# A two-layer block kernel: per-layer gates computed with tokens on the partitions in two token blocks, their normed rows turned back, and the first shared values moved ahead of the keys

## The chip, the core and the metric

The kernel runs on one NeuronCore of a Trainium2 chip. The metric is device time in microseconds from one launch to its end, so lower is better. Five instruction streams run beside each other and meet only at semaphores: TensorE (matmul), VectorE, ScalarE, GpSimd, and SyncE, which here only issues DMAs. Each stream is strictly in order: an instruction that waits holds everything behind it.

## What is computed

The kernel runs two blocks of a small language model over 256 tokens (272 with 16 meta tokens in the first block) of width 1024, batch 1, all in float32. The change touches the second block only. Per layer i that block does:

```python
for i in range(2):
    h = rms_norm(x, g_pre_mix[i])
    if i == 0:
        mix = short_conv_mixer(h, ...)
    else:
        k, v = shared_kv(x, g_kv, w_kv)     # rms_norm(x, g_kv) @ w_kv, split in keys and values
        mix = diff_attention(h, k, v, ...)  # 8 heads, two softmaxes a head, subtracted
    x = x + rms_norm(mix, g_post_mix[i])
    ffn = conv_ffn(rms_norm(x, g_pre_ffn[i]), ...)   # up to 2 * 2816, causal conv of width 3, silu gate, down
    x = x + rms_norm(ffn, g_post_ffn[i])
    gate = sigmoid(rms_norm(x, g_pre_ple[i]) @ w_gate[i])          # 1024 x 1024
    x = x + rms_norm(gate * (p[i] @ w_proj[i]), g_post_ple[i])     # p[i]: 256 tokens x 256
```

Weights come in float32 and are used as a rounded high part plus a remainder, and so are the activations: each product is three matmuls (high weight with high activation, high with low, low with high).

## The kernel before

**Layout.** The residual `X` and the normed inputs `UH` (high) and `UL` (low) have features on the partitions and tokens along the free axis. A root mean square is taken outside the products: the gain is applied in `split_hi`/`split_lo` (line 540), the products run on the unnormed rows, and the token's reciprocal root is multiplied in when a product is evicted. `root_begin`, `root_sum` and `root_end` sum squares over the partitions with one-column matmuls (line 462), `root_sqrt` (line 506, ScalarE) and `root_recip` (line 513, VectorE) make the reciprocal, `root_spread` (line 520) spreads it over all partitions, `root_keep` (line 528) copies it. `preload` (line 532) evaluates a function on one column so that its table is loaded early. `keep_going` (line 402) runs products of ones on TensorE that nobody reads.

**Weights.** All weights are one stream of units of up to 128 x 1024, in the order of `weight_units`. SyncE loads unit n into one of four `RAW` buffers as soon as unit n-4 has been split. ScalarE (`act_split`, line 346) rounds it into one of seven `WH` buffers, once the unit seven before has been marked `used` by TensorE; VectorE (`dve_split`, line 353) makes the remainder `WL`. TensorE waits for `wl`. The places of all splits in the two streams are written out by hand. `products` (line 368) makes one 128-row output tile of 24 matmuls, 256 tokens wide; `first_products` (line 413) makes four such tiles side by side, k by k, so that it can follow the arrival of `UL` k by k.

**PSUM banks.** The eight PSUM banks are handed out by the class `Banks`, in the order in which TensorE's stream is written. `take` gives the next bank round the ring, skipping one that is held, and makes TensorE wait for the event that frees the bank's last contents; `put` names the bank itself and waits in the same way. `root_banks` takes two neighbours and marks the second as free after `root_sqrt` (`rs`). `hold` keeps the first of the pair out of the ring until the next `root_sum`; `go_on` moves the ring's place. In `tensor_ffn` this place matters:

```python
elif u == 2:
    # m == 0: b = banks.take(...)            then root_sum takes two banks
    # m == 1: b = banks.put(t, banks.at["root", prev], ...)
...
if (u, m) == (3, 0):
    banks.go_on((banks.at["root", prev] + 1) % 8)
```

Tile (u, m) of the up projection is evicted by VectorE into `FZ` (line 2322, event `fz`), in order (0,0), (0,1), (1,0) and so on, between weight splits and the convolution's taps. Before, in layer 0, the pair of the root of `sco` is in banks 6 and 7, the five embedding tiles of `embed(0, 5)` in 0 to 4, the first four up tiles in 5, 7, 0 and 1, tile (2,0) in 2, the root of `ffn0` in 3 and 4, tile (2,1) in 6 and tile (3,0) in 5.

**The per-layer embedding.** `embed(j0, j1)` in `tensor_ffn` makes the tiles of p @ w_proj: tiles 0 to 4 at the entrance of the feed-forward, 5 to 7 before the gate. ScalarE copies them to `MM2` (line 2176). Then the gate runs as four pairs of feature tiles: VectorE multiplies by the reciprocal root (line 2349), ScalarE takes the sigmoid (line 2247), VectorE multiplies by `MM2` (line 2355), ScalarE squares. The norm of the result is the start of the next stage: `tensor_diff` (layer 0) or `tensor_end` (layer 1) fills with `keep_going`, sums, spreads, and `add_normed` (lines 1902 and 1905) or `vector_end` (lines 2817 and 2819) adds to `X`.

**Keys, values and attention.** `tensor_diff` makes the eight key tiles first, four of them by `first_products`, with the root of `kv`; then a loop over eight steps s does query s, the scores of head s-1, `value(s)` (line 2450, half of a 256-column value block), and attention of head s-2. VectorE multiplies keys and queries by the root on eviction (lines 2676 and 2694). After the loop the output projection makes its first four tiles in banks 0 to 3 and takes the next banks round the ring for the other four; ScalarE squares (line 1858) and copies (line 1860) each output tile.

## Time and profile before

| what | us |
|---|---|
| three timed executions | 1263.52, 1260.85, 1262.09 |
| their median | 1262.09 |
| span of the profiled execution | 1261.9 |
| TensorE busy in it | 1231.6 (98%) |
| VectorE busy | 908.1 (72%) |
| ScalarE busy | 737.1 (58%) |
| mean granted TensorE clock | 0.994 of full speed |

The span runs from the first to the last instruction of the profiled execution; it is 0.2 us from the median of the timed ones. A timeline row reads: start, duration, engine, line, operation, output and inputs, shapes, count, and in brackets the idle time ahead of it with the engine that ended it. Matmuls are pipelined, so the duration of one is longer than its distance to the next; the distance is what it costs. On the page, the line of a group gives its busy time and the mean duration of one instruction in ns.

### The profile page before, as it was taken

How to read it: one execution, taken by the hardware profiler on the slowest of the kernel's cores; microseconds unless marked ns; L12 is line 12 of the kernel's file. 1: busy time of each engine (PE TensorE's matmuls, PEld its weight loads, DVE VectorE, ACT ScalarE, POOL GpSimd, SP SyncE). 2: the span in 40 equal slices, each digit the busy share in tenths (PEclk: the TensorE clock that was granted, in tenths of full speed). 3: DMA queues.
4: the chain of work that ended last, by engine and by line, in shares of the span. 5: the costliest groups of instructions: out<-in, count | busy, mean ns of one | idle time of the engine just before them, and what ended most of it. 6: DMA issues, size and time to landing. Idle time of an engine off the chain costs nothing.

```text
span 1261.9 us, 24318 instructions
## 1 busy us (share of the span) xinstructions
PE 1231.6 (98%) x10110; PEld 1206.4 (96%) x10110; DVE 908.1 (72%) x1571; ACT 737.1 (58%) x1257; POOL 6.4 (1%) x16
## 2 busy tenths in 40 slices
PE   8999999999999999999999999999999999999997
PEld 8889799999999999999999999999888899999997
DVE  6896566665446776444876899966788768999656
ACT  6753456664445765334555666655766866665655
POOL 1000000000000000000000000000000000000000
PEclk9999999999999999999999999999899999999999
DMA  7223244555552655553663666574364236665640
GB/s 275 72 101 105 64 164 148 192 181 180 174 168 98 216 186 185 184 184 126 218 195 119 193 194 199 159 238 134 120 225 159 89 117 192 193 189 188 215 141 34
DMA packets 59753, 205.51 MB, mean 163 GB/s; under 512 B 6739, under 2 KB 9340, under 8 KB 59516
## 3 DMA queue, kind: packets, MB, share of 16 engines
q1 hardware_dynamic: 57536, 201.21, 49.0%
q10 hardware_dynamic: 2108, 2.75, 0.7%
q8 instruction: 80, 1.31, 0.4%
q14 instruction: 29, 0.24, 0.1%
HBM read 202.87 MB, written 1.06 MB: 162 GB/s over the span
## 4 chain that ended last, share of the span: by engine, by line
PE 85%; DVE 8%; ACT 4%; issue 1%; DMA 1%; DVEq 0%; ACTq 0%
PE PS L368 69%; PE PS L413 6%; DVE WL L353 2%; PE PS L380 2%; DMA RAW<-wpack 1%; ACT WH L346 1%; PE PS L462 1%; PE PS L2450 1%; ACT EE L2608 1%; PE PS L520 1%; PE PS L2517 0%; PE PS L688 0%; DVE X L1905 0%; ACT L532 0%; PE PS L402 0%
## 5 line engine op out<-in xcount | busy, mean ns | idle before, releaser
L353 DVE TENSOR_TENSOR WL<-RAW,WH 128x1024 fp32r<-128x1024 f32 (+2 forms) x387 | 460.6, 1195 | 211.3 <-ACT WH L346 210.8
L346 ACT ACTIVATE WH<-RAW 128x1024 fp32r<-128x1024 f32 (+2 forms) x387 | 392.3, 1033 | 218.6 <-PE PS L368 184.8
L368 PE MATMUL PS<-UH,WH 128*128 128x256 f32 (+1 forms) x1464 | 415.7, 284 | 7.6 <-DVE WL L353 3.8
L368 PE MATMUL PS<-UL,WH 128*128 128x256 f32 (+1 forms) x1464 | 414.9, 283 | 0.0
L368 PE MATMUL PS<-UH,WL 128*128 128x256 f32 (+1 forms) x1464 | 414.7, 283 | 0.0
L368 PEld LDWEIGHTS PS<-UH,WH 128*128 128x128 f32 x1464 | 276.6, 189 | 8.6 <-issue 3.4
L368 PEld LDWEIGHTS PS<-UH,WL 128*128 128x128 f32 x1464 | 276.9, 189 | 0.0
L368 PEld LDWEIGHTS PS<-UL,WH 128*128 128x128 f32 x1464 | 275.2, 188 | 0.0
L368 PE MATMUL PS<-HL,WH 128*128 128x272 f32 (+1 forms) x512 | 145.8, 285 | 0.0
L368 PE MATMUL PS<-HH,WH 128*128 128x272 f32 (+1 forms) x512 | 145.6, 284 | 0.0
L368 PE MATMUL PS<-HH,WL 128*128 128x272 f32 (+1 forms) x512 | 145.4, 284 | 0.0
L368 PE MATMUL PS<-FH,WH 128*128 128x256 f32 x352 | 98.5, 280 | 0.0
L368 PE MATMUL PS<-FL,WH 128*128 128x256 f32 x352 | 98.5, 280 | 0.0
L368 PE MATMUL PS<-FH,WL 128*128 128x256 f32 x352 | 98.5, 280 | 0.0
L368 PEld LDWEIGHTS PS<-HH,WL 128*128 128x128 f32 x512 | 96.6, 189 | 0.0
L368 PEld LDWEIGHTS PS<-HL,WH 128*128 128x128 f32 x512 | 96.3, 188 | 0.0
L368 PEld LDWEIGHTS PS<-HH,WH 128*128 128x128 f32 x512 | 96.1, 188 | 0.0
L413 PE MATMUL PS<-UH,WH 128*128 128x256 f32 (+1 forms) x240 | 68.7, 286 | 1.5 <-DVE UL L540 1.2
L413 PE MATMUL PS<-UL,WH 128*128 128x256 f32 (+1 forms) x240 | 67.6, 282 | 0.0
L413 PE MATMUL PS<-UH,WL 128*128 128x256 f32 (+1 forms) x240 | 67.6, 282 | 0.0
L368 PEld LDWEIGHTS PS<-FH,WH 128*128 128x128 f32 x352 | 66.2, 188 | 0.0
L368 PEld LDWEIGHTS PS<-FL,WH 128*128 128x128 f32 x352 | 66.2, 188 | 0.0
(409 smaller groups left out, 2066.1 us busy)
## 6 DMA issues: line engine op xcount, KB each, us to landing
RAW<-wpack SPq DMA_DIRECT2D x361, 512.0 KB, 4.2
RAW<-wpack SPq DMA_DIRECT2D x18, 384.0 KB, 3.5
RAW<-wpack SPq DMA_DIRECT2D x6, 256.0 KB, 2.7
C<-cst SPq DMA_DIRECT2D x1, 1072.0 KB, 5.9
HB<-bias_rows ACTq DMA_DIRECT2D x1, 1024.0 KB, 5.3
out<-X SPq DMA_DIRECT2D x4, 256.0 KB, 2.3
X<-xin ACTq DMA_DIRECT2D x2, 272.0 KB, 6.0
X<-xin SPq DMA_DIRECT2D x2, 272.0 KB, 5.9
```

The source lines that it names most:

```text
L346: a.e.activation(WH[n % NH][:, 0:w], RAW[n % NR][:, 0:w], ACT.Copy).then_inc(*a.mark("wh", n))
L353: v.e.tensor_tensor(WL[n % NH][:, 0:w], RAW[n % NR][:, 0:w], WH[n % NH][:, 0:w].bitcast(f32), ALU.subtract).then_inc(*v.mark("wl", n))
L368: ins = t.e.matmul(o, part(n, hw, kw, a, b), x(kx), start=first and not i and not p, stop=last and i == len(kcs) - 1 and p == 2)
L380: ins = t.e.matmul(o, x(kx), part(n, hw, kw, 0, w), start=not i and not p, stop=i == len(kcs) - 1 and p == 2)
L413: ins = t.e.matmul(PS[:, b, 0:w], part(n, hw, k, 0, 128), x_(k), start=k == 0 and p == 0, stop=k == 7 and p == 2)
L462: return t.e.matmul(o, src[:, m, a:z], ONE[:, 0:1], start=start, stop=stop)
L520: ins = t.e.matmul(PS[:, b, a:z], rooted(st, x).to_broadcast([128, 128]), ID[:, 0:z - a], start=True, stop=True)
L2450: ins = t.e.matmul(PS[:, b, 0:256], x[:, k, 128 * i:128 * i + 128], part(n, hw, kw, 0, 256), start=k == 0 and p == 0, stop=k == 7 and p == 2)
L2608: ins = a.e.activation(e, e, ACT.Exp, bias=s[:, 2 * i + m:2 * i + m + 1], scale=-1.0, accum_out=s[:, 4 + 2 * i + m:5 + 2 * i + m])
```

## The change

- **Units.** The gate's weights come as eight units of two k-slices x 512 columns instead of eight of eight k-slices x 128 columns. The first 512 value columns come as four such units ahead of the keys; keys 4 to 7 take the places of value halves 0 to 3 in the loop. The embedding's weights are cut at columns 512 and 768.
- **Embedding.** `embed` uses 128 tokens as the stationary operand and 256 features as the moving one; six tiles instead of five are made at the entrance of the feed-forward, two instead of three before the gate. `MR` is the token-major view of `MM2`.
- **Gate.** Tokens on the partitions: the reciprocal root becomes the per-partition scale of the sigmoid, which reads PSUM directly. Columns 0 to 511 of both token blocks are made side by side, with `root_sum` after k = 5 of 8; then columns 512 to 1023 of block 0, then of block 1. The sum of squares comes from accumulators on ScalarE and VectorE. Root, reciprocal and scaling of block 0 follow while TensorE makes block 1, and `gate_turned` turns the normed rows of block 0 back with eight transposes, placed inside the products of block 1. `gate_added` multiplies by the gain and adds to `X`.
- **Layer 0's follow-up.** `tensor_diff` begins with the value products of block 0, in which the transposes of block 1 stand ahead of k = 6; then the value products of block 1, the bias product, and keys 0 to 3. Fillers, sum and spread of the root of `ple0` are gone.
- **Layer 1's end.** Block 1's second half is made in two column halves; its reciprocal root goes into a diagonal matrix with which eight matmuls turn and scale at once. The output leaves in eight DMAs of 128 KB instead of four of 256 KB.

The core of the diff:

```diff
         else:
-            proj("k", "w_kv_2", None, 0, 1024)
-            for g in range(4):
-                for m in range(2):
-                    proj("q", "w_q_2", 0, 256 * g + 128 * m, 256 * g + 128 * m + 128)
-                    u.append(("v", "w_kv_2", None, list(range(4 * m, 4 * m + 4)), cols(1024 + 256 * g, 1280 + 256 * g)))
+            pairs_of_rows("v", "w_kv_2", None, 1024, 1536)
+            proj("k", "w_kv_2", None, 0, 512)
+            for h in range(8):
+                proj("q", "w_q_2", 0, 128 * h, 128 * h + 128)
+                if h < 4:
+                    proj("k", "w_kv_2", None, 512 + 128 * h, 640 + 128 * h)
+                else:
+                    m, c = h % 2, 1024 + 256 * (h // 2)
+                    u.append(("v", "w_kv_2", None, list(range(4 * m, 4 * m + 4)), cols(c, c + 256)))
...
             root_spread(t, prev, S)
-            embed(2, 5)
+            embed(2, 6)
...
             root_end(t, f"f{layer}", 1, S)
-            embed(5, 6)
+            embed(6, 7)
             root_spread(t, f"f{layer}", S)
-            embed(6, 8)
-            keep_going(t, 2, f"f{layer}")
+            embed(7, 8)
+            keep_going(t, 8, f"f{layer}")
...
+            def gate_rows(h, k, blocks_, c0=0, c1=512):
+                n, kw = n0 + 4 * h + k // 2, k % 2
+                t.wait_ge("wl", n)
+                t.wait_ge("ul", st, k)
+                for i in blocks_:
+                    if k == 0:
+                        banks.take(t, ("gate", layer, i, h, c0), ("sig", layer, i, h, int(c1 == 512)))
...
+            for k in range(8):
+                n = gate_rows(0, k, (0, 1))
+                if k == 5:
+                    root_sum(t, st, 0, S, ("rs", st))
             for u in range(4):
+                sig.also(("used", n0 + u), ("gate", layer, 1, 0, 0))
+            for k in range(8):
+                gate_rows(1, k, (0,))
+            if layer == 0:
+                for k in range(8):
+                    if k == 6:
+                        gate_turned(t, layer, 0)
+                    gate_rows(1, k, (1,))
...
+            gate_sigmoid(a, layer, 0, 0, 0, 512)
+            gate_sigmoid(a, layer, 1, 0, 0, 512)
+            act_split(a, n0 + NH + 2)
             gate_square(0)
+            act_split(a, n0 + NH + 3)
             gate_square(1)
+            act_split(a, n0 + NH + 4)
+            gate_sigmoid(a, layer, 0, 1, 0, 512)
+            preload(a, ACT.Sqrt, 61)
+            gate_root(a, layer, 0)
+            preload(a, ACT.Sigmoid, 62)
+            gate_scale_first(a, layer, 0)
...
         def tensor_diff(t):
-            keep_going(t, 10)
-            root_begin(t, "ple0", 1, S, ("mr", "kv", 6))
-            banks.hold(("root", "ple0"))
-            keep_going(t, 8)
-            root_end(t, "ple0", 1, S)
-            root_spread(t, "ple0", S)
+            for i in range(2):
+                b = banks.take(t, ("v", 0, i), ("v", 0, i))
+                for k in range(8):
+                    if (i, k) == (0, 6):
+                        gate_turned(t, 0, 1)
...
+            spare = banks.at["nt", 0, 0]
+            b = banks.put(t, spare, ("gr",), ("gr0",))
...
+            for j in range(4):
+                key(j, banks.take(t, ("k", j), ("kh", j)) if j != 2 else banks.put(t, spare + 1, ("k", j), ("kh", j)))
+                if j == 1:
+                    root_sum(t, "kv", 0, S, ("rk", "kv"))
+                if j == 2:
                     root_spread(t, "kv", S)
...
+                if s < 4:
+                    key(4 + s, banks.put(t, BV + s % 2, ("k", 4 + s), ("kh", 4 + s)))
+                    return
...
+            parts(0, 0, 4)
+            gate_product(v, 0, 1, 1, 0, 512)
+            gate_squares(v, 0, 1)
+            dve_split(v, n0)
+            parts(0, 4, 6)
+            gate_recip(v, 0, 1)
+            gate_scale_second(v, 0, 1)
+            parts(0, 6, 8)
+            dve_split(v, n0 + 1)
+            parts(1, 0, 8)
...
-            key(0)
-            key(1)
-            dve_split(v, n0 + NH + 2)
-            key(2)
-            key(3)
-            dve_split(v, n0 + NH + 4)
-            for j in range(4, 8):
+            for j in range(4):
                 key(j)
+                dve_split(v, n0 + NH + 1 + j)
```

On ScalarE the squares of `kv`, the copy of the bias row, the eight query inputs (`XH`) with four weight splits among them, `root_sqrt` of `kv`, `root_keep` and then the two copies of the first values follow in this order. `parts(i, a, b)` is, per feature tile, `gate_added` and then the low part of the key and value input; its high part is on ScalarE.

## Rows read from the trace of the kernel before

**Rows 1.** The page: busy time of the engines, the two costliest groups

```profile
PE 1231.6 (98%) x10110; PEld 1206.4 (96%) x10110; DVE 908.1 (72%) x1571; ACT 737.1 (58%) x1257; POOL 6.4 (1%) x16
...
L353 DVE TENSOR_TENSOR WL<-RAW,WH 128x1024 fp32r<-128x1024 f32 (+2 forms) x387 | 460.6, 1195 | 211.3 <-ACT WH L346 210.8
...
L346 ACT ACTIVATE WH<-RAW 128x1024 fp32r<-128x1024 f32 (+2 forms) x387 | 392.3, 1033 | 218.6 <-PE PS L368 184.8
```

**Rows 2.** TensorE's timeline at the first convolved feed-forward: start us, us, engine, line, operation

```profile
679.93 0.36 PE L413 MATMUL PS<-UH,WH 128*128 128x256 f32 x1
...
697.99 0.28 PE L368 MATMUL PS<-UH,WH 128*128 128x256 f32 x1
...
701.81 0.36 PE L368 MATMUL PS<-UH,WH 128*128 128x256 f32 x1 [0.82 <-DVE WL L353]
```

**Rows 3.** Timelines there, then of the second layer: VectorE's evictions into FZ, TensorE

```profile
697.18 0.76 DVE L2322 TENSOR_TENSOR FZ<-PS,RR 128x256 f32<-128x256 f32 x2 [1.31 <-ACT RR L528]
...
708.95 0.41 DVE L2322 TENSOR_TENSOR FZ<-PS,RR 128x256 f32<-128x256 f32 x1
...
1059.70 0.41 DVE L2322 TENSOR_TENSOR FZ<-PS,RR 128x256 f32<-128x256 f32 x1
...
1052.57 0.36 PE L368 MATMUL PS<-UH,WH 128*128 128x256 f32 x1 [0.82 <-DVE WL L353]
```

**Rows 4.** ScalarE's timeline there: two copies of embedding tiles

```profile
680.36 0.64 ACT L2176 ACTIVATE MM<-PS 128x256 f32<-128x256 f32 x2
```

**Rows 5.** The gate stage of layer 0, timelines of TensorE and VectorE

```profile
873.69 0.36 PE L413 MATMUL PS<-UH,WH 128*128 128x256 f32 x1 [0.59 <-DVE UL L540]
...
885.37 0.58 PE L462 MATMUL PS<-ONE,ACC 128*128 128x1 f32 x4
...
884.79 0.43 DVE L449 TENSOR_TENSOR ACC<-ACC 128x256 f32<-128x256 f32 x1
...
890.06 0.69 DVE L2355 TENSOR_TENSOR MM<-MM,TMA 128x512 f32<-128x512 f32 x1
```

**Rows 6.** The same stage on ScalarE, timeline

```profile
886.26 1.28 ACT L532 ACT_TABLE_LOAD   x1
...
887.56 0.20 ACT L532 ACTIVATE SMALL<-EPS 128x1 f32<-128x1 f32 x1
...
889.40 1.29 ACT L2247 ACTIVATE TMA<-TMA 128x512 f32<-128x512 f32 x2
```

**Rows 7.** TensorE's timeline elsewhere: 512-column products, four transposes and the product after

```profile
148.73 0.39 PE L380 MATMUL PS<-WH,CL 128*128 128x512 f32 x1
...
148.95 0.39 PE L380 MATMUL PS<-WL,CH 128*128 128x512 f32 x1
...
987.61 0.60 PE L2490 MATMUL PS<-ID,MM 128*128 128x128 f32 x4
...
987.97 0.37 PE L368 MATMUL PS<-XH,WH 128*128 128x256 f32 x1
```

**Rows 8.** TensorE's timeline after the gate of layer 0

```profile
925.44 0.71 PE L520 MATMUL PS<-ID,RS 128*128 128x128 f32 x4 [1.61 <-DVE RS L513]
...
934.92 0.39 PE L368 MATMUL PS<-XH,WH 128*128 128x256 f32 x1
...
941.20 0.39 PE L368 MATMUL PS<-XH,WH 128*128 128x256 f32 x1 [0.47 <-DVE QH L2694]
```

**Rows 9.** Table by stretch: busy per engine, then granted clock, DMA share, GB/s

```profile
898.70:902.10 3.40, 2.62 (x24) 2.45 (x22) 2.87 (x10) 2.50 (x6) 0.00 (x0) 1.00 0.05 12
...
905.50:908.90 3.40, 3.40 (x14) 2.63 (x13) 3.15 (x7) 2.28 (x5) 0.00 (x0) 0.50 0.49 162
```

**Rows 10.** Attention's output tiles, timelines of TensorE and ScalarE

```profile
1013.77 0.28 PE L368 MATMUL PS<-UH,WH 128*128 128x256 f32 x1
...
1017.39 0.50 ACT L1860 ACTIVATE M<-PS,G 128x256 f32<-128x256 f32 x1
```

**Rows 11.** VectorE's timeline: the kernel's last addition

```profile
1258.41 0.69 DVE L2819 TENSOR_TENSOR X<-X,MM 128x512 f32<-128x512 f32 x1
```

More of the change, by code:

```diff
@@ L36, in rows, with pairs_of_rows @@
                 u.append((key, name, idx, list(range(k, k + 4)), cols(c, c + 256)))
+    def pairs_of_rows(key, name, idx, a, b):
+        for c in range(a, b, 512):
+            for k in (0, 2, 4, 6):
+                u.append((key, name, idx, [k, k + 1], cols(c, c + 512)))
     def blocks(n):
@@ L2089, in embed @@
                 for j in range(j0, j1):
-                    x, j_, last = (0, 0, 3) if j < 4 else (1, 4, 4) if j < 5 else (2, 5, 7)
-                    n, at = unit_at["ple", 3 * layer + x], 128 * (j - j_)
+                    i, x, at = j % 2, (0, 0, 1, 2)[j // 2], (0, 256, 0, 0)[j // 2]
+                    n = unit_at["ple", 3 * layer + x]
                     b = banks.take(t, ("ple", layer, j), ("pe", layer, j))
-                    products(t, PS[:, b, 0:S], n, [(0, 0), (1, 1)], at, at + 128,
-                             lambda k: PH[:, k, :], lambda k: PL[:, k, :], lambda k: ("ul", "p", layer)).then_inc(
-                                 *t.mark("ple", layer, j))
-                    if j == last:
+                    t.wait_ge("wl", n)
+                    t.wait_ge("ul", "p", layer)
+                    for k in range(2):
+                        for p, (y, hw) in enumerate(((PH, 1), (PL, 1), (PH, 0))):
+                            ins = t.e.matmul(PS[:, b, 0:256], y[:, k, 128 * i:128 * i + 128], part(n, hw, k, at, at + 256),
+                                             start=k == 0 and p == 0, stop=k == 1 and p == 2)
+                    ins.then_inc(*t.mark("ple", layer, j))
+                    if j in (3, 5, 7):
                         sig.also(("used", n), ("ple", layer, j))
@@ new lines, in gate_rows @@
+            def gate_rows(h, k, blocks_, c0=0, c1=512):
+                n, kw = n0 + 4 * h + k // 2, k % 2
+                t.wait_ge("wl", n)
+                t.wait_ge("ul", st, k)
+                for i in blocks_:
+                    if k == 0:
+                        banks.take(t, ("gate", layer, i, h, c0), ("sig", layer, i, h, int(c1 == 512)))
+                    b = banks.at["gate", layer, i, h, c0]
+                    for p, (x, hw) in enumerate(((UH, 1), (UL, 1), (UH, 0))):
+                        ins = t.e.matmul(PS[:, b, c0:c1], x[:, k, 128 * i:128 * i + 128], part(n, hw, kw, c0, c1),
+                                         start=k == 0 and p == 0, stop=k == 7 and p == 2)
+                    if k == 7:
+                        ins.then_inc(*t.mark("gate", layer, i, h, c0))
+                return n
@@ new lines, in tensor_ffn, with gate_turned @@
+            for u in range(4, 8):
+                sig.also(("used", n0 + u), ("gate", layer, 1, 1, 256 * layer))
+        def gate_turned(t, layer, i):
+            b = banks.take(t, ("nt", layer, i), ("x2", AFTER[layer], i, 7), 2)
+            t.wait_ge("m", f"ple{layer}", i)
+            t.wait_ge("mr", f"ple{layer}", i)
+            for j in range(8):
+                ins = t.e.transpose(PS[:, b + j // 4, 128 * (j % 4):128 * (j % 4) + 128], MR[:, i, 128 * j:128 * j + 128], ID[:, :])
+                if j % 4 == 3:
+                    ins.then_inc(*t.mark("nt", layer, i, j // 4))
@@ L2254, in last_step @@
-            def last_step():
-                ple = f"ple{layer}"
-                for m in range(2):
-                    a.wait_ge("gz", layer, 3, m)
-                    a.e.activation(TMA[:, 2 + m, 0:S], TMA[:, 2 + m, 0:S], ACT.Sigmoid).then_inc(*a.mark("sig", layer, 3, m))
-                a.wait_ge("acc", ple, 1)
-                a.free["sq", 1] = ("sum", ple)
-                for m in range(2):
-                    a.wait_ge("pg", layer, 3, m)
-                    a.e.activation(SQ[1][:, m, 0:S], MM2[:, 6 + m, :], ACT.Square).then_inc(*a.mark("sq", ple, 3, m))
-                sig.also(("sq", ple, 3), ("sq", ple, 3, 1))
@@ L2567, in scalar_diff @@
             root_sqrt(a, "kv", S)
-            act_split(a, n0 + NH + 1)
             root_keep(a, "kv", 0, S)
-            act_split(a, n0 + NH + 4)
+            a.wait_ge("rr", "kv")
+            for i in range(2):
+                a.wait_ge("dif", "v", 0, i)
+                a.e.activation(V[:, i, 0:512], PS[:, banks.at["v", 0, i], :], ACT.Copy, scale=rooted("kv", 1 + i)).then_inc(
+                    *a.mark("v", 0, i))
+            act_split(a, n0 + 4 + NH)
             scalar_embed(a, 1)
```

313 lines of the change are left out of this document (175 added, 138 removed).

## The prediction

> **What bounds the kernel now.** I read the page first: TensorE is busy 98% of the span, VectorE 72%, ScalarE 58% [rows 1]. So TensorE's own work sets the time, and a change pays only if it takes work or idle time from TensorE. Next I read TensorE's waits and its timeline. They show few gaps: 0.82 us at each feed-forward entrance [rows 2, 3], 0.59 us ahead of the gate [rows 5], 1.61 and 0.47 us around keys and queries [rows 8]. The larger loss is hidden in the busy time: after each gate the stream holds fillers, one-column sums and a spread instead of products. In layer 0 this fills the ten microseconds of [rows 9], and there the granted clock falls to 0.50, from 2.4 to 1.2 GHz, after a stretch in which TensorE was busy 2.62 of 3.40 us, partly with one-column sums. The change aims at this, and at the tail, where VectorE ends at 1259.10 [rows 11]. Last I went through the diff for every wait that TensorE gets, which includes the hand-out of PSUM banks: a stream with 98% busy loses what it waits.
>
> **Part 1, the sixth embedding tile at the entrance of the feed-forward.** It looks free: one tile of six matmuls changes places. But it takes a bank. Counting on from front: the root of `sco` stays in 6 and 7 (6 held), the embedding now takes 0 to 5, the first four up tiles 7, 0, 1, 2, tile (2,0) bank 3, the root of `ffn0` 4 and 5, and `put` places tile (2,1) in 6. The hold has just ended, so the ring gives tile (3,0) the next bank: 6 again. Before it was 5, whose contents had left at 697.5. Now (3,0) waits for the eviction of (2,1). The sixth FZ eviction in VectorE's order is that one, at 708.95, ended 709.36 [rows 3], while TensorE is ready for (3,0) at 697.99 [rows 2]. Two smaller shifts come on top: tile (1,1) now lies in bank 2 and waits for the copy of embedding tile 2, the first of the pair at 680.36, so the products begin at 680.8 and not at 679.93 [rows 2, 4]; of these 0.9 us, 0.7 stay, and the spread, root copy and evictions follow TensorE, so they shift too. Then (3,0) starts at 710.2 and (3,1) one tile later. A tile is 24 matmuls at 0.12 us (96 of them fill 873.69 to 885.37 [rows 5]), 2.85 us: 713.05, against 701.81 [rows 2], which already holds the old 0.82 us wait. **Cost 11.2 us.** Nothing gives it back: behind this point TensorE runs without a gap and the splits it needs are even further ahead. The second layer repeats it if the root of `do` and the embedding lie the same way. By my count `lam` ends in bank 1, so attention's last output tiles take 2 to 5, that root 6 and 7, the embedding again 0 to 5. With 1059.70 and 1052.57 [rows 3] the sum is 1059.70 + 0.41 + 0.7 + 0.1 + 2.85 - 1052.57 = **11.2 us.**
>
> **Part 2, gate of layer 0 to the first query.** I laid the new order out by hand on the three engines from 873.69 on. A 512-column matmul costs 0.23 us [rows 7] against two of 0.12, so 96 in the gate and 48 for the values save about 1 us in all. Eight transposes cost 0.8 us (0.36 for four [rows 7]); sigmoid, copies and squares of 512 columns 0.65, a table load with its dummy 1.46 [rows 6], a product of 512 columns 0.69 [rows 5], a weight split 1.03 on ScalarE and 1.2 on VectorE [rows 1]. The 128-token additions and remainders are not in the trace; 0.3 us each is my estimate, between half of and the whole 0.41 of 256 columns [rows 3]. The waits that result on TensorE:
> - `root_sum` after k = 5 is reached at 882.2, but needs the sum of squares, which ends at 885.22 [rows 5]. Before, it stood behind k = 7 and waited for next to nothing. **3.1 us.** The first half ends at 888.6.
> - The transposes of block 0 need its scaling. On ScalarE, behind the end of the first half, stand a split, two sigmoids, two squares, three more splits, the third sigmoid and two table loads around the root: ready at 900.2. **1.9 us.** The gate ends at 902.5.
> - Value product k = 4 of block 0 needs a remainder on VectorE that stands behind block 1's product, its squares and a split, and an input on ScalarE behind split, sigmoid and table load: 908.4. **3.2 us.**
> - Block 1 of the values starts behind one more split on both: 913.8. **1.8 us.** Values, bias product, keys 0 and 1 then run to 925.9.
> - Key 2 is put in the second bank of the root pair, which `root_sqrt` frees. That stands on ScalarE behind eight query inputs and four splits, at 929.0. **2.9 us.**
> - Key 3 takes bank 0, held by the first values; their copy stands behind `root_keep`. **1.2 us.**
> - The first query takes the bank of key 3, whose eviction stands on VectorE behind three splits: 939.9. **2.8 us.**
>
> The first query starts at 939.9, before at 934.92; the second, without its old 0.47 us wait, at 945.7 against 941.20 [rows 8]. By then both kernels have done the same number of products, since the loop does keys where it did values. **Cost 4.5 us** at full clock; all the new waits, 17 us, eat the ten microseconds of filler and more. The loop itself I cost at nothing: one key eviction of 0.41 us a step [rows 3] replaces a copy on ScalarE, on an engine that is 72% busy [rows 1]; uncovered, four of them would be 1.6 us. ScalarE's DMA of the bias rows is issued later, about 929, and is first needed after 945. SyncE's loads wait on splits as before, and the waits only give them time.
>
> **Part 3, attention's output.** Output tile 4 now takes bank 2, still full of tile 2, and before a bank that had long been empty. TensorE is there at 1013.77, the copy of tile 2 ends at 1017.89 [rows 10]. **4.1 us.**
>
> **Part 4, the tail.** Layer 1's gate starts 350.76 us after layer 0's, at 1224.45 (701.81 and 1052.57 give that distance [rows 2, 3]). It has the same 3.1 us wait, but no splits behind it. Its chain ends: second half of block 0 at 20.5 us from its start, its scaling at 25.9, last products at 28.3, then sigmoid, product, squares, table load, root, reciprocal, diagonal and the first pair of turning matmuls, and eight additions: 33.1. Before: 1259.10 - 1224.45 = 34.65. **Gain 1.6 us.** The eight output DMAs carry as much in rows half as long; only the last counts, and I take it at nothing (bounds: 0 and 1 us more).
>
> **Part 5, the clock.** In a low stretch the same products take twice as long; before, the low stretch of [rows 9] cost next to nothing, since little useful ran in it. The new waits stand ahead of products on the critical path. Eight of them are between 1.9 and 11.5 us long. I take six falls at 1.5 us each, **9 us**; bounds 0 and 16 us (eight times 2).
>
> The Trainium skill (ScalarE: Activation LUTs, What ACT_TABLE_LOAD costs) puts a drain of 1.38 us behind each load of 1.28. The rows disagree: the load at 886.26 is followed by an ACTIVATE at 887.56 [rows 6], so the trace decides. With the page's figure the chain to the transposes would be 2.8 us longer and the tail 2.8 us longer, and the sum 1306.
>
> **Sum.** 1261.9 + 11.2 + 11.2 + 4.5 + 4.1 - 1.6 + 9 = 1300.3; the profiled span lies 0.2 us below the median, so I say 1300.5 us. With the bounds of the clock, and 3 us either way on the hand-laid part 2, this case runs from 1289 to 1310.
>
> **Rivals.**
> - **Only the ring count in the feed-forward is wrong** (tile (3,0) finds an empty bank in both layers). Then part 1 is the 0.7 us shift twice, and two falls of the clock go: 1300.5 - 21 - 3 = 1276.5. Against it: the count reproduces every bank of before that I can follow in the code.
> - **Faster.** Every result is there when TensorE asks. This decides if the scaling of block 0 is ready within 4.2 us after its second half and remainders come faster than 0.69 us per k. TensorE's work between 873.69 and the first query is then 144 products of 512 columns (33.1), four keys (11.4), sixteen transposes (1.6) and sums, bias and spread (2.6), 48.7 us against 61.2: gain 12.5, and 4.7 at the tail with `root_sum`'s wait gone: 1245. Against it: the sum of squares ends at 885.22 in any order [rows 5], and the splits stand where they are written.
> - **No change.** No bank wait binds anywhere, but the waits on ScalarE and VectorE do. By my layout the first query then comes 0.2 us early and the tail 1.6 early, against 1.4 at the entrances and 1 or 2 for the clock: 1262.
>
> **Chances.** Forecast 0.80, wrong count 0.07, faster 0.06, no change 0.07. A difference under 0.2%, some 2.5 us, can't be told from none here. Faster by more gets 0.08, within 0.05, slower 0.87. The range must leave no more than 0.2 outside: from 1274, which takes in the wrong count, to 1311.
>
> **What would show it.** In the trace of after: a TensorE gap near 11 us in each feed-forward, ended by FZ (line 2322), is the main step; without it the forecast is out by 20 us or more. Gaps ended by the sum of squares near 882, by ScalarE's root ahead of key 2, by VectorE's key eviction ahead of the first query, and by ScalarE's copy near the output's tile 4 show the others. A last addition about 34.65 - 33.1 us nearer to the last gate's start shows the tail. If none of the gaps is there, I have misread the ring; if they are there and the time is near 1290, only the clock was oversized.

## The result, and the profile after

| | before | after |
|---|---|---|
| timed executions, median (lowest to highest) | 1261.70 (1260.85 to 1263.52) | 1306.32 (1305.47 to 1307.47) |
| ratio, 95% interval | | 1.035 (1.0338 to 1.0362) |
| span of the profiled execution | 1261.9 | 1305.3 |
| TensorE busy in it | 1231.6 (98%) | 1241.1 (95%) |
| granted TensorE clock | 0.994 | 0.979 |

The changed kernel is 44.6 us slower, 43.4 us by the spans of the two profiles. The forecast was 1300.5 us, with a range of 1274 to 1311.

The first view is that of TensorE's waits, whole span: engine and line, what it waited for, us in total, times, longest. Lines of the changed kernel lie 9 to 42 further down, and those of VectorE in attention some 100: 2364 is the eviction into `FZ`, 377 is in `products`, 471 is the one-column sum, 2466 the value products, 2210 the transposes, 2783 the eviction of the keys.

```profile
PE PS L377 <- DVE FZ L2364: 22.5, 2, 11.3
PE PS L471 <- DVE ACC L458: 5.6, 2, 2.8
PE PS L377 <- ACT M L1873: 5.2, 1, 5.2
PE PS L2466 <- DVE UL L549: 3.9, 2, 2.6
PE PS L377 <- ACT RS L515: 3.2, 1, 3.2
PE PS L377 <- DVE M L2783: 2.6, 1, 2.6
PE PS L2210 <- ACT MM L2326: 2.6, 2, 2.0
...
PE PS L377 <- ACT V L2653: 1.1, 1, 1.1
```

Each of these rows is new. Before, the longest wait at these places was the 1.61 us of [rows 8]. The timeline of TensorE gives their places (start, duration, engine, line, operation, and in brackets the idle time ahead with what ended it); only rows with such a wait are shown:

```profile
680.55 0.36 PE L422 MATMUL PS<-UH,WH 128*128 128x256 f32 x1 [0.47 <-ACT MM L2223]
709.88 0.58 PE L377 MATMUL PS<-UH,WH 128*128 128x256 f32 x1 [11.26 <-DVE FZ L2364]
886.55 0.47 PE L2175 MATMUL PS<-WH,UH 128*128 128x512 f32 x1 [0.55 <-issue]
898.27 0.64 PE L471 MATMUL PS<-ONE,ACC 128*128 128x1 f32 x4 [2.82 <-DVE ACC L458]
914.99 1.26 PE L2210 MATMUL PS<-ID,MM 128*128 128x128 f32 x8 [1.96 <-ACT MM L2326]
924.36 0.47 PE L2466 MATMUL PS<-WH,UH 128*128 128x512 f32 x1 [2.58 <-DVE UL L549]
929.63 0.50 PE L2466 MATMUL PS<-WH,UH 128*128 128x512 f32 x1 [1.36 <-DVE UL L549]
945.60 0.38 PE L377 MATMUL PS<-UH,WH 128*128 128x256 f32 x1 [3.19 <-ACT RS L515]
951.72 0.38 PE L377 MATMUL PS<-UH,WH 128*128 128x256 f32 x1 [1.05 <-ACT V L2653]
957.76 0.39 PE L377 MATMUL PS<-XH,WH 128*128 128x256 f32 x1 [2.63 <-DVE M L2783]
...
1039.97 0.55 PE L377 MATMUL PS<-UH,WH 128*128 128x256 f32 x1 [5.21 <-ACT M L1873]
1060.22 0.36 PE L422 MATMUL PS<-UH,WH 128*128 128x256 f32 x1 [0.47 <-ACT MM L2223]
1089.55 0.58 PE L377 MATMUL PS<-UH,WH 128*128 128x256 f32 x1 [11.26 <-DVE FZ L2364]
1265.87 0.47 PE L2175 MATMUL PS<-WH,UH 128*128 128x512 f32 x1 [0.53 <-issue]
1277.60 0.56 PE L471 MATMUL PS<-ONE,ACC 128*128 128x1 f32 x2 [2.81 <-DVE ACC L458]
```

Rows 680.55, 709.88 and 886.55 answer to [rows 2, 5], row 945.60 and the two behind it to [rows 8], row 1089.55 to the one of [rows 3] at 1052.57. The last additions are VectorE's, which answer to [rows 11]:

```profile
1300.72 2.16 DVE L2428 SCALAR_TENSOR_TENSOR X<-PS,G,X 128x128 f32<-128x128 f32 x8 [0.87 <-PE PS L2908]
```

From such starts I cut the span in stages. A stage runs from the first product of one part to the first of the next (a feed-forward's starts at its first up tile); the kernels named `sixth`, `ring` and `lam` are experiments told below. All in us.

| stage | before | after | `sixth` | `ring` | `lam` |
|---|---|---|---|---|---|
| start to feed-forward 0 | 679.9 | 680.6 | 683.1 | 679.4 | 680.3 |
| feed-forward 0 to its gate | 193.8 | 206.0 | 206.4 | 193.6 | 193.6 |
| gate 0 to the first query | 61.2 | 71.2 | 61.3 | 66.7 | 57.8 |
| first query to feed-forward 1 | 95.7 | 102.5 | 102.7 | 95.1 | 97.1 |
| feed-forward 1 to its gate | 193.8 | 205.7 | 205.6 | 193.6 | 193.6 |
| gate 1 to the end of the last addition | 34.7 | 37.0 | 35.2 | 33.9 | 31.2 |
| last addition to the end | 2.8 | 2.4 | 2.8 | 2.3 | 2.3 |
| span | 1261.9 | 1305.3 | 1297.0 | 1264.6 | 1255.8 |

24 of the 43 us are lost in the two feed-forward stages, in which the change does little but make one embedding tile earlier.

### The profile page after: what moved, and what is told of

It reads as the page before. It is cut to its first block, busy times and chain, and to the rows that moved or that the text cites. A ratio compares the mean times of both kernels' runs of the same rounds, so it can differ in the third digit from the quotient of the medians.

```text
span 1305.3 us, 23858 instructions
## 1 busy us (share of the span) xinstructions
PE 1241.1 (95%) x9877; PEld 1204.2 (92%) x9877; DVE 908.6 (70%) x1590; ACT 739.7 (57%) x1255; POOL 6.4 (0%) x16
## 4 chain that ended last, share of the span: by engine, by line
PE 82%; DVE 9%; ACT 7%; issue 2%; DMA 0%; ACTq 0%; DVEq 0%
PE PS L377 67%; PE PS L422 4%; DVE WL L362 3%; ACT WH L355 2%; PE PS L389 2%; PE PS L2175 2%; ACT L541 1%; DVE UL L549 1%; PE PS L471 1%; DVE X L1918 1%; ACT UH L545 1%; ACT EE L2693 1%; DVE M L1915 1%; PE PS L529 0%; PE PS L2585 0%
## 5 line engine op out<-in xcount | busy, mean ns | idle before, releaser
L355 ACT ACTIVATE WH<-RAW 128x1024 fp32r<-128x1024 f32 (+2 forms) x387 | 396.4, 1035 | 272.4 <-PE PS L377 241.0
L377 PE MATMUL PS<-UH,WH 128*128 128x256 f32 (+1 forms) x1432 | 410.7, 287 | 36.8 <-DVE FZ L2364 22.5
L377 PE MATMUL PS<-UL,WH 128*128 128x256 f32 (+1 forms) x1432 | 409.2, 286 | 0.0
L377 PE MATMUL PS<-UH,WL 128*128 128x256 f32 (+1 forms) x1432 | 409.0, 286 | 0.0
L377 PEld LDWEIGHTS PS<-FH,WL 128*128 128x128 f32 x352 | 66.2, 188 | 0.0
L545 ACT ACTIVATE UH<-X,G 128x256 fp32r<-128x256 f32 (+2 forms) x84 | 37.5, 484 | 28.5 <-DVE X L1918 18.0
L2364 DVE TENSOR_TENSOR FZ<-PS,RR 128x256 f32<-128x256 f32 x88 | 36.8, 420 | 14.5 <-PE PS L377 11.9
```

The source lines that it names most:

```text
L355: a.e.activation(WH[n % NH][:, 0:w], RAW[n % NR][:, 0:w], ACT.Copy).then_inc(*a.mark("wh", n))
L377: ins = t.e.matmul(o, part(n, hw, kw, a, b), x(kx), start=first and not i and not p, stop=last and i == len(kcs) - 1 and p == 2)
L545: a.e.activation(hi, src, ACT.Copy, scale=gc).then_inc(*a.mark("uh", *key))
L2364: v.e.tensor_tensor(FZ[layer][(2 * u + m) % 4][:, :], PS[:, banks.at["ffn", layer, u, m], 0:S], RR[0][:, 0:S], ALU.mult).then_inc(*v.mark( ...
```

## The experiments

**One tile alone, in the kernel before.** `sixth` takes from the change the cut of the embedding's weights and the order of its tiles, and nothing else:

```diff
-        for c, z in ((0, 512), (512, 640)):
+        for c, z in ((0, 512), (512, 768)):
...
-            embed(2, 5)
+            embed(2, 6)
...
-            embed(5, 6)
+            embed(6, 7)
             root_spread(t, f"f{layer}", S)
-            embed(6, 8)
+            embed(7, 8)
```

> The kernel before with one thing of the change alone: six embedding tiles at the entrance of each feed-forward and two before each gate; gates, values, keys and tail stay as they were. My theory: the sixth tile takes a bank, tile (3,0) of the up projection falls on the bank of tile (2,1) and waits some 11 us in both layers, 12 with the slow clock behind it; the ring also stays one bank behind, so that output tile 4 of attention falls on bank 2, still full of tile 2, which costs 5 to 7 us. 1262 + 24 + 6 = 1292 us. If the tile only costs its wait at the entrances, 1286. Rival (the time of the changed kernel comes from the reordered gate and values, the tile is just six matmuls that change places): 1262 within 2 us.

Measured: 1296.87 us, ratio 1.0276 (1.0259 to 1.0293), 5 us over the expected 1292. TensorE's waits begin with

```profile
PE PS L368 <- DVE FZ L2321: 22.5, 2, 11.3
PE PS L368 <- ACT M L1860: 5.2, 1, 5.2
```

They are the same two rows, to the tenth, as those of the whole change. So the tile makes both gaps of the feed-forwards and also the gap at attention's output, with gates, values and keys of the old kind. The stage table shows it: both feed-forwards and the stage between them are those of after, within 0.4 us, and gate 0 to the first query is that of before. The first stage is 3.1 us longer than before in this profile. About 2.0 us of it are there by the matching row of TensorE at 188.41 us (186.38 before), long before anything that the edit touches, so they are spread between executions, and the profiled one, 1299.16 us, is the slowest of the four; the other 1.1 are the sixth tile itself and a wait of 0.51 us for ScalarE's copy behind it. So the first stage explains little of what the expected 1292 was short. The stage before feed-forward 1 grew by 7.0 us and both feed-forwards by 24.4, where 6 and 24 were expected.

**The ring set on one tile earlier, in the changed kernel.** `ring`:

```diff
                     for m in range(2):
+                        if (u, m) == (3, 0):
+                            banks.go_on((banks.at["root", prev] + 1) % 8)
                         b = banks.take(t, ("ffn", layer, u, m), ("fz", layer, u, m))
...
-                        if (u, m) == (3, 0):
-                            banks.go_on((banks.at["root", prev] + 1) % 8)
```

> The changed kernel with the ring of banks set on before tile (3,0) of the up projection and not after it, so that the tile gets the bank of tile (0,0), evicted first. My theory: both gaps of 11.26 us and the slow clock behind them go; the stretches from the feed-forward's entrance to the gate fall from 206.0 and 205.7 us to 193.8, so 1306.3 - 24.1 = 1282 us. Rival (a later up tile only waits in its place, since VectorE's evictions are the bound): a gap of over 5 us a few tiles later, and 1295 us or more.

Measured: 1268.29 us, ratio 1.0053 (1.0038 to 1.0068). TensorE's longest waits are now

```profile
PE PS L471 <- DVE ACC L458: 5.7, 2, 2.8
PE PS L2466 <- DVE UL L549: 3.8, 2, 2.4
PE PS L377 <- ACT RS L515: 3.1, 1, 3.1
PE PS L377 <- DVE WL L362: 3.0, 3, 1.3
PE PS L2210 <- ACT MM L2326: 2.6, 2, 2.0
```

The edit gave back 38.0 us where I expected 24.1: the expectation missed by 14. Three rows are gone, not one: `FZ` (22.5), `M` at line 1873 (5.2, output tile 4) and `M` at line 2783 (2.6, the key ahead of the first query). With tile (3,0) in bank 7 the tile behind it goes to bank 0, and what the ring hands out later stands one bank further on, or two where pairs and the held bank make it skip one. Output tile 4 then takes bank 4 again, as before the change, and key 3 takes bank 2 where it took bank 0, so that the first query no longer lands on it. An offset that starts with one bank made 22.5 + 5.2 + 2.6 = 30.3 us of waits; since the old 0.82 us for weights comes back in both layers, 28.7 net. The rest of the 38 is the slow clock behind the waits (the profile's mean clock is 0.997, against 0.979) and the spread between executions: the profiled execution, 1266.45 us, is the fastest of the four. No later up tile waits instead, so the rival is out.

The Trainium skill (Perfetto Trace Analysis, Matmuls) says that independent groups should rotate through different banks so that an eviction overlaps the next products. The trace agrees only in part: both kernels rotate, and the order of the rotation decided over 30 us of waits.

**The bank of output tile 4 set by hand**, `ring_do`, on top of `ring`:

```diff
+            banks.go_on(4)
             tensor_output(t, "mix", "do", ("mr", "ffn1", 6), uh, ul, o_ready, first=2)
```

> The kernel with the ring set on before tile (3,0), and besides the ring set to bank 4 ahead of output tile 4 of attention, so that tiles 4 to 7 don't wait for the copy of tile 2. My theory: the 5.21 us wait goes, and with it the slow stretch of 6.8 us around it: 5 to 7 us less than with the first edit alone, 1275 to 1277 us. Rival (the tile would have waited for its normed rows or its weights anyway): within 1.5 us of the first edit alone.

Measured: 1270.38 us, ratio 1.0068 (1.0053 to 1.0083), against 1.0053 (1.0038 to 1.0068) without. The expectation missed, and for the reason just told: in `ring` the wait was already gone and the tile already in bank 4. So `go_on(4)` moves nothing: every tile has the same bank as in `ring`, and the two programs are the same, instruction by instruction. The run tests neither the theory nor the rival. It shows the spread instead: the medians of four executions each of one program lie 2.1 us apart, the spans of two profiles of it 2.4 (1264.6 and 1267.0), the stages gate 0 to the first query 0.6 (66.7 and 67.3) and the last gates 1.6 (33.9 and 35.5). TensorE's wait for the sum of squares, first in `ring`, then in `ring_do`, and a stretch behind each, in the same order:

```profile
884.72 0.58 PE L471 MATMUL PS<-ONE,ACC 128*128 128x1 f32 x4 [2.84 <-DVE ACC L458]
```

```profile
884.73 0.58 PE L471 MATMUL PS<-ONE,ACC 128*128 128x1 f32 x4 [2.82 <-DVE ACC L458]
```

```profile
884.70:899.80 15.10, 13.19 (x58) 10.50 (x58) 10.94 (x21) 12.86 (x21) 0.00 (x0) 1.00 0.66 212
```

```profile
886.50:889.70 3.20, 3.20 (x9) 2.52 (x8) 1.56 (x2) 0.61 (x2) 0.00 (x0) 0.50 0.52 156
```

In a stretch row stand its length, the busy us and count of TensorE's matmuls, its weight loads, VectorE, ScalarE and GpSimd, then the granted clock (1.00 and 0.50 here), the DMA share and GB/s. The same wait in the same program was followed by a fall of the clock in one execution and by none in the other.

**The wait kept, the clock kept up.** `fill` is the changed kernel with products nobody reads in the gap:

```diff
                 elif u > 2:
                     for m in range(2):
+                        if (u, m) == (3, 0):
+                            t.wait_ge("fz", layer, 0, 0)
+                            keep_going(t, 90, done=("ffn", layer, 0, 0))
                         b = banks.take(t, ("ffn", layer, u, m), ("fz", layer, u, m))
```

> The changed kernel with 90 products of ones, 10.7 us at 0.12 us each, in the wait ahead of tile (3,0), in both layers; the wait itself stays as long. If the fall of the clock costs what the slow stretches in the trace say (4.4 and 3.7 us at half speed behind the waits, half of it lost), the time falls by 4 us to 1302 and the granted clock stays at 2.4 GHz there. If the clock costs nothing, 1306 within 1 us. If the fillers themselves delay the tile, over 1307.

Measured: 1301.26 us, ratio 1.0317 (1.0301 to 1.0332); the tile starts at 709.71, as late as without the fillers. The view of busy time by stretch shows what they change (columns as above). First the changed kernel, the gap and what follows it, then `fill`:

```profile
698.60:709.88 11.28, 0.03 (x1) 0.00 (x0) 8.90 (x14) 8.21 (x15) 0.00 (x0) 0.59 0.50 176
709.88:714.30 4.42, 4.42 (x20) 4.42 (x21) 2.83 (x5) 1.44 (x2) 0.00 (x0) 0.50 0.67 209
```

```profile
698.60:709.70 11.10, 10.64 (x89) 10.44 (x87) 8.89 (x14) 8.04 (x15) 0.00 (x0) 1.00 0.52 168
709.70:714.30 4.60, 4.59 (x38) 4.59 (x39) 3.56 (x7) 2.84 (x4) 0.00 (x0) 1.00 0.76 220
```

Behind the gap, 20 products in 4.42 us at a clock of 0.50 (1.2 GHz), against 38 in 4.60 us at 1.00 (2.4 GHz). The feed-forward stages shrink to 204.0 us each (from 680.37 to 884.40, and from 1058.73 to 1262.76), by 2.0 and 1.6. So a fall of the clock behind these long waits has a price of its own of 1.6 to 2 us, and busy time hides it: TensorE counts as 100% busy in the second row. The fillers show 3.6 of the 5 us. The rest lies above all in the last stage, 35.5 us against 37.0, where this profile has a shorter low stretch; no edit stands there, and `ring` and `ring_do` differ by as much in it.

**The sum after k = 7**, `sum_late`, on top of `ring`:

```diff
-                if k == 5:
+                if k == 7:
                     root_sum(t, st, 0, S, ("rs", st))
```

> The kernel with the ring set on before tile (3,0) (1268.3 us), and besides the sum of squares of both gates asked for after k = 7 and not after k = 5. Reckoned by the wait alone, the 2.8 us go twice: 1262.7. But my theory is that TensorE only reaches the next wait sooner: the first half then ends at about 885.4 and the root's table load (885.6 to 887.1) still stands ahead of ScalarE's next split, so that its chain to the scaling of block 0 starts 1.1 us sooner and not 2.8; the transposes then wait 1.96 + 1.7 us. Layer 0 gains 1.1, the last gate 1 to 2.8, the clock may give or take 1.7: 1264.5 to 1266.5. Rival (all of it comes back): 1262.7.

Measured: 1263.41 us, ratio 1.0011 (1.0002 to 1.0021). That is 1.1 us below my range and 0.7 above the rival's 1262.7. In layer 0 the mechanism of my theory held. The wait for the sum is gone, and the transposes' is longer; they start 26.05 us behind the gate's start, only 0.8 sooner than in `ring` (26.88):

```profile
898.93 1.06 PE L2210 MATMUL PS<-ID,MM 128*128 128x128 f32 x8 [3.49 <-ACT MM L2326]
```

Its stage is 66.4 us (872.88 to 939.25) against 66.7 in `ring` and 67.3 in `ring_do`: of 2.8 us, 0.4 to 1.0 stayed. The last gate has no chain of splits and gained 2.2 or 3.8 (1227.77 to 1259.40, 31.6 against 33.9 and 35.5). By medians the gain over `ring` is 4.9 us, by spans 2.8, or 5.2 against the span of `ring_do`; the profile of `ring` lies low in its own runs, so 2.8 is the least. Layer 0 gave little; most of the gain, and its spread, is in the last gate.

**Keys and the root of `kv`**, `keys`, on top of `sum_late` (with the line of `ring_do`):

```diff
-                key(j, banks.take(t, ("k", j), ("kh", j)) if j != 2 else banks.put(t, spare + 1, ("k", j), ("kh", j)))
+                key(j, banks.take(t, ("k", j), ("kh", j)) if j < 2 else
+                    banks.put(t, banks.at["nt", 0, 1] + j - 2, ("k", j), ("kh", j)))
...
-            b = banks.take(t, ("lam",), ("lame",))
+            b = banks.put(t, spare + 1, ("lam",), ("lame",))
...
                 if j % 2:
                     act_split(a, n0 + 4 + j // 2)
+                if j == 5:
+                    root_sqrt(a, "kv", S)
```

(`root_recip` is moved in the same way on VectorE.)

> As with the later sum, and besides: root_sqrt and root_recip of kv stand behind the sixth and not the eighth query input, keys 2 and 3 take the banks of block 1's transposes, and the sum over lambda takes the second bank of the first transposes. My theory: the waits of key 2 (3.1 us, ScalarE's root) and key 3 (1.05 us, copy of the values) go, and nothing is late behind them: 4.2 us less than with the later sum alone, about 1261. Rival (the spread behind key 2 or the first query waits in their place): less than 2 us off.

Measured: 1265.17 us, ratio 1.0024 (1.0014 to 1.0033), where I expected 1261: 1.8 us slower than without. The first query comes sooner, 59.2 us behind the gate's start (873.05 to 932.24) against 66.4. Key 4, which neither the theory nor the rival named, then gives it back:

```profile
940.50 0.58 PE L377 MATMUL PS<-UH,WH 128*128 128x256 f32 x1 [5.25 <-ACT SMALL L2661]
```

I had put the two columns for lambda in the bank that key 4 takes, and ScalarE reads them (its `Exp`) behind the copies of the values, four splits with 3.6 us of waiting for their weights, the next embedding's input and a table load. With the slow clock behind it the stage up to feed-forward 1 is 102.4 us against 95.0. My own edit was the fault of the first kind again: a bank handed to a tile whose former contents leave late.

**One table load off the chain**, `turned`, on top of `keys`:

```diff
             gate_root(a, layer, 0)
-            preload(a, ACT.Sigmoid, 62)
             gate_scale_first(a, layer, 0)
+            preload(a, ACT.Sigmoid, 62)
```

> As with the earlier root of kv, and besides the scaling of block 0's first half stands ahead of the sigmoid's table load and not behind it, in both gates. A table load with its dummy takes 1.5 us, the transposes of block 0 wait for it, so this wait falls by 1.5 us in layer 0: about 1259.5. If a load is followed by a drain of another 1.38 us, as the Trainium skill has it (ScalarE: Activation LUTs, What ACT_TABLE_LOAD costs), nearly 3 us go; if the following wait, for remainders of block 0 behind the sigmoid of block 1, takes all, within 0.5 us of the run without.

Measured: 1262.84 us, ratio 1.0004 (0.9994 to 1.0014), 2.3 us under `keys` by medians and 0.9 by spans, where 1.5 was expected. The transposes start 24.8 us behind the gate's start (872.95 to 897.75) and not 26.0 (873.05 to 899.01), 1.2 us sooner. ScalarE's rows of the changed kernel have the price of a load:

```profile
912.31 0.29 ACT L2321 ACTIVATE RS<-SMALL 128x1 f32<-128x1 f32 x1 [0.54 <-DVE SMALL L2412]
912.62 1.28 ACT L541 ACT_TABLE_LOAD   x1
...
913.91 0.20 ACT L541 ACTIVATE SMALL<-EPS 128x1 f32<-128x1 f32 x1
914.02 0.70 ACT L2326 ACTIVATE MM<-MM,RS 128x512 f32<-128x512 f32 x1
```

Load, dummy and scaling stand 1.29 and 0.11 us apart. The drain of 1.38 us that the Trainium skill adds (ScalarE: Activation LUTs, What ACT_TABLE_LOAD costs) is in neither the rows nor the 1.2 us by which the transposes come sooner.

**The lambda columns elsewhere**, `lam`, on top of `turned`:

```diff
                 query(s)
+                if s == 0:
+                    lam()
```

where `lam()` is the former two-column product, now in the bank of key 0.

> As with the scaling ahead of the table load (1262.8), and besides the two-column product for lambda stands behind the first query and takes the bank of key 0, so that key 4 in the loop no longer takes a bank that ScalarE's Exp of lambda has to leave first. That wait was 4.78 us on TensorE, with 3.4 us at half speed around it. My theory: both go and nothing is late behind, 6 us less: 1256 to 1258 us, faster than the kernel before by 0.4%. Rival (key 5 or query 1 waits for weights or an eviction in its place, since ScalarE stood idle for loads of weights up to 2.4 us at that place): 1260 us or more.

Measured: 1257.64 us, ratio 0.9962 (0.995 to 0.9975): 5.2 us less, and faster than the kernel before. What TensorE waits for most is now small:

```profile
PE PS L2466 <- DVE UL L549: 3.3, 1, 3.3
PE PS L377 <- DVE WL L362: 3.0, 3, 1.3
PE PS L2210 <- ACT MM L2326: 2.3, 1, 2.3
PE PS L377 <- DVE QH L2803: 1.9, 1, 1.9
```

The last row is part of the rival: query 1 waits 1.89 us until VectorE has evicted query 0, behind evictions of keys and their splits. So one of the six us came back.

**Splits moved out of the chain.** Two tries; ScalarE's part of each, with VectorE's splits moved to match. First `lean`, on top of `turned` (v2 and v3 follow ahead of and behind block 1's sigmoid):

```diff
-            act_split(a, n0 + NH + 2)
             gate_square(0)
-            act_split(a, n0 + NH + 3)
             gate_square(1)
-            act_split(a, n0 + NH + 4)
+            act_split(a, n0 + NH + 2)
             gate_sigmoid(a, layer, 0, 1, 0, 512)
...
             preload(a, ACT.Sigmoid, 62)
+            act_split(a, n0 + NH + 3)
```

> As with the scaling ahead of the table load, and besides three weight splits of each engine that stand inside the chain to the scaling of block 0 and inside the one to the remainders k = 4 to 7 are moved behind it or into idle time. My theory: the transposes of block 0 no longer wait, the remainders cost 1 to 2 us in all and not 3.9, and the stretch from the gate to the first query is 52 to 54 us against 66.7 with the ring alone and 61.2 before; the whole is 1254 to 1257 us, faster than the kernel before. Rival (a moved split is late at its own product, VectorE's remainder of value unit 2 or 3): within 1 us of the run without.

Measured: 1264.85 us, ratio 1.0022 (1.0013 to 1.0031), 2.0 us slower than `turned`. The transposes' wait fell from 2.2 to 0.8, but v1's split came so late that the additions of block 0 stood behind it: VectorE idled 2.73 us for it, and the value products waited 5.6 us instead of 3.3.

```profile
898.75 1.23 DVE L362 TENSOR_TENSOR WL<-RAW,WH 128x1024 fp32r<-128x1024 f32 x1 [2.73 <-ACT WH L355]
```

That is the rival of this run in kind, a moved split that is late; the expected stretch of 52 to 54 us from the gate to the first query was 60.9.

Then `lean2`, on top of `lam`, which puts the splits into the idle places of the trace of `lean` (besides, the last of the four moves behind the table load for block 1's root):

```diff
             act_split(a, n0 + NH + 2)
             gate_square(0)
-            act_split(a, n0 + NH + 3)
             gate_square(1)
-            act_split(a, n0 + NH + 4)
+            act_split(a, n0 + NH + 3)
             gate_sigmoid(a, layer, 0, 1, 0, 512)
...
             gate_scale_first(a, layer, 0)
+            act_split(a, n0 + NH + 4)
             preload(a, ACT.Sigmoid, 62)
```

> As the run before, and besides the weight splits inside the two chains of the gate's end are put where ScalarE and VectorE stood idle: unit v0 between the first sigmoids and the squares, v1 behind the squares, v2 behind the scaling and ahead of the sigmoid's table load, v3 behind the root's table load. My theory: the transposes of block 0 wait 1.1 us and not 2.2, the remainders of block 0 2 to 3 us and not 3.3: 1 to 2 us less than the run before, 1254.5 to 1257. Rival (each split only moves the wait to the next k of the values): within 0.7 us of the run before.

Measured: 1257.87 us, ratio 0.9961 (0.9947 to 0.9974), no different from `lam`. TensorE's timeline shows why (only rows with a wait are shown):

```profile
896.46 1.06 PE L2210 MATMUL PS<-ID,MM 128*128 128x128 f32 x8 [0.88 <-ACT MM L2326]
900.12 0.47 PE L2466 MATMUL PS<-WH,UH 128*128 128x512 f32 x1 [1.20 <-DVE UL L549]
905.05 0.47 PE L2466 MATMUL PS<-WH,UH 128*128 128x512 f32 x1 [1.92 <-DVE UL L549]
908.35 0.47 PE L2466 MATMUL PS<-WH,UH 128*128 128x512 f32 x1 [0.79 <-DVE UL L549]
911.54 0.47 PE L2466 MATMUL PS<-WH,UH 128*128 128x512 f32 x1 [1.56 <-DVE UL L549]
```

These are 6.35 us in five pieces; `lam` had 5.5 us in two. The rival held. Product, squares, root, scaling, transposes, addition and remainders of each block follow one another on two engines, and the products of the other block don't cover them. Whether another order of the work could, I haven't tried.

## Why the prediction was right, point by point

**The feed-forwards (part 1).** Right in place, bank and size. The cost forecast was 11.2 us a layer. In layer 0 the wait is 11.26 us where 11.5 was forecast; less the old 0.82, plus the 0.6 us by which the stage starts later (680.55 against 679.93), that is 11.1. It ends with the eviction that was named, the sixth into `FZ`:

```profile
709.41 0.42 DVE L2364 TENSOR_TENSOR FZ<-PS,RR 128x256 f32<-128x256 f32 x1
```

`sixth` shows that the tile alone makes the wait. The stages grew by 12.2 and 11.9 us, the clock included.

**Gate to first query (part 2).** All seven waits are there, in the forecast order and with the forecast releasers:

| wait | forecast | measured |
|---|---|---|
| `root_sum` on the squares | 3.1 | 2.82 |
| transposes on the scaling | 1.9 | 1.96 |
| values, k = 4 of block 0 | 3.2 | 2.58 |
| values, block 1 | 1.8 | 1.36 |
| key 2 on the root | 2.9 | 3.19 |
| key 3 on the values' copy | 1.2 | 1.05 |
| first query on key 3 | 2.8 | 2.63 |

Their sum, 15.6, is close to the 16.9 forecast. The step named the bank of the last one rightly, but did not see that it is the same offset of the ring as in part 1; `ring` removed it without touching VectorE.

**Attention's output (part 3).** Right in place, 1.1 us short: 4.1 forecast, 5.21 measured. The loop ran 1.8 us faster than before up to this tile (1039.97 - 5.21 - 957.76 = 77.0 us behind the first query, against 1013.77 - 934.92 = 78.85 [rows 8, 10]), so TensorE came to the full bank sooner; the forecast had costed the loop at nothing. The step took it as a fact of its own; it is the sixth tile's third bill.

**The tail (part 4).** Forecast 33.1 us from the gate's start to the last addition; `ring`, without a low clock there, has 33.9, so the mechanism is right and 0.8 us short; the same program with a low stretch, `ring_do`, has 35.5. In the changed kernel it is 37.0. Its own row and that of `ring`, the stretch of 6.8 us behind the wait for the sum, show the difference:

```profile
1277.50:1284.30 6.80, 6.70 (x18) 5.48 (x19) 2.42 (x3) 2.22 (x5) 0.00 (x0) 0.50 0.00 0
```

```profile
1240.10:1246.90 6.80, 6.78 (x32) 5.63 (x33) 4.27 (x6) 4.34 (x7) 0.00 (x0) 1.00 0.00 1
```

18 products at 1.2 GHz against 32 at 2.4 GHz.

**The clock (part 5)** is the term that was mis-sized: 9 us forecast, some 14 measured. I take what each stage grew beyond its forecast growth, or beyond its measured wait. The feed-forwards: 11.26 us of wait less the old 0.82 [rows 2] is 10.4, so 12.2 - 10.4 = 1.8 and 11.9 - 10.4 = 1.5. Gate to first query: 71.2 - 61.2 = 10.0, of which 5.0 were forecast (939.9 - 934.92), leaves 5.0 (and up to 6.3, since the seven waits came out 1.3 short). First query to feed-forward 1: 6.7, less 5.2 of wait, plus 1.5 for two old waits that are gone (0.47 ahead of the second query [rows 8], 1.01 at 951.90), leaves 3.0. The tail: 37.0 - 33.9 (as in `ring`) = 3.1. Together 14.4 us, inside the bounds of 0 to 16. With 14 for 9 the sum is 1305.3, where the span is; that proves nothing, since 14.4 is what the other terms leave over. The granted clock gives a count that does not lean on the forecast: TensorE worked at 0.50 for 4.4 and 3.6 us behind the `FZ` waits, three times 3.35 us between the gate and the first query, 5.3 us at the output and 6.8 us in the tail. At 2.4 GHz the same products would take half of these 30.2 us, so the falls cost 15.1 us at most. The number of falls was near the forecast six (one behind each `FZ` wait, three between the gate and the first query, one each at the output and in the tail make seven); the average price of 1.5 us was too low, since the low stretches at the output and in the tail lasted 6.8 us and the two behind the `FZ` waits cost up to 2 us.

**What was luck.** The parts missed both ways: the seven waits are 1.3 us under the forecast, the output 1.1 and the tail 0.8 over it, and the clock 5 over. The prediction's other sum, 1306 with a drain behind each table load, lies nearest to the measured 1306.32, and by chance: in the changed kernel the load at 912.62 ends at 913.90, and the next ACTIVATE starts at 913.91. Two readings are a little off, by some 0.2 us in the sum: a load with its dummy takes 1.50 us by [rows 6], not 1.46, and tile (3,0)'s 24 products at the distance of [rows 5], 11.68 us for 96, take 2.92, not 2.85.

**The rivals.** That the count of banks was wrong is refuted by the `FZ` rows. "Faster" was priced by two conditions: scaling ready in time and fast remainders. Both stayed unmet even in `lean2`, so it was rightly low. But with the offset gone and the waits of keys and lambda sorted, the change does gain: `lam` is 0.38% faster than before (0.25 to 0.5%). From the gate to the first query it needs 57.8 us against 61.2, and the tail 31.2 against 34.7; 1.3 us are given back in the loop. So the idea can be worth some 5 us, but not by one bank alone: with the bank mended (`ring`) it is still 0.5% slower than before, and the rest came from the later sum, the banks of keys and lambda, and the table load.

## What to carry to other kernels

When buffers are handed out by a ring in program order, an extra tile costs nothing where it is added and everything where the count no longer fits what leaves late; write out the bank of every tile behind the change, to the end of the kernel, and compare it with the list of before. The same list of the kernel with an edit shows an edit that changes nothing, as `ring_do`, ahead of the run. Undo the cause before its symptoms: here four waits for banks, at three kinds of places, looked like three separate costs and were one offset. But the offset was not all: four further edits were needed before the change gained anything. Behind a wait on TensorE look at the granted clock: busy time shows nothing of the 1.6 to 5 us that a stage loses there.

## What the runs showed of the hardware

- The clock fell to 1.2 GHz not only behind the gaps of 11.26 us. In `turned` and `lam` the wait of 2.2 us ahead of the transposes left it at 2.4 GHz and the one of 3.3 us, 8.5 us later, was followed by a fall; in `lean2` five waits of 0.8 to 1.9 us in the same place brought none, with a mean clock of 1.0 over the span. So five short waits brought no fall where two longer ones of less time in all brought one, in these executions; `lean2` was no faster for it. No wait of a given length settles it: the 2.84 us ahead of the sum of squares brought none in `ring`, and 2.82 in `ring_do`, the same program, did.
- The same stretch of the same program lasted 1.4 us longer in one profile than in another, with a fall of the clock in it that the other lacks (the row at 886.50 above): the transposes stand 26.9 us behind the gate's start in `ring` (872.99 to 899.87) and 28.3 in `ring_do` (873.00 to 901.32).
